# Sums of squares of k and q: ScalarE's accumulated squares against products with a column of ones

## The chip, the cores and the metric

One core of a Trainium2 chip runs the whole kernel. The metric is the device time of one execution in microseconds (us), here the median of three runs. Everything is in fp32; the large projections are made of split operands (fp32r), three products for one.

## What is computed

The reference is one layer with two request groups, 128 context tokens and 1024 latent tokens, which the kernel keeps side by side as nine chunks of 128 tokens (in rows of 1154 columns, with a gap of two between the groups). After an input projection it has a gated DeltaNet with 8 heads and an RG-LRU with 8 blocks. What the change touches is this part:

```python
def l2norm(x):
    return x * lax.rsqrt(jnp.sum(x * x, axis=-1, keepdims=True) + EPS)

def delta_branch(...):
    qkv = jax.nn.silu(short_conv(qkv, conv_w)).astype(jnp.float32)
    q, k, v = jnp.split(qkv.reshape(bsz, t, 3, N_DN_HEADS, DN_HEAD_DIM), 3, axis=2)
    q, k, v = l2norm(q[:, :, 0]), l2norm(k[:, :, 0]), v[:, :, 0]
```

For every token and head the sums of the 128 squares of k and of q are needed, with the tokens on the partitions, since the scales derived from them are applied to rows of tokens.

## The kernel before

**Layout.** k, q and v of a head are kept channel by channel: the 128 channels of the head on the partitions, the tokens along the row (`kT`, `qT`, `v_conv`, 1154 columns each). TensorE turns them to tokens chunk by chunk (`turn`, L741): three chunks to a PSUM bank, nine in all for one tensor, into banks 2, 3 and 4.

**Order of a head.** The loop over heads runs `joins(h)`, `scan(h)`, `phase_a(h)` on TensorE, ScalarE and VectorE, each engine with its own queue in order and with counted semaphores between them; one `phase_a(-1)` stands before the loop, so it runs eight times. `scan` goes through the nine chunks and is filled with projections of the next head. `phase_a` makes the next head's scores while TensorE does the other projections; meanwhile VectorE inverts 32 x 32 blocks (L1583 to L1592). `joins` combines the blocks.

**Sums of squares before.** In `phase_a` ScalarE copies the turned k to `ktok` (L1096) and squares each turned chunk from PSUM with a running sum (L1100), 9 squares, each followed by a readout of its accumulator. q is turned for nothing but this (L798): ScalarE squares its nine chunks with a running sum (L1143). The sums, `ssk` and `ssq`, go to VectorE (L1546 and L1631).

**Names in the steps.** L746 is the transposes, L784 the scores of phase_a, L673 to L675 the projections, L763 and L868 the products of the RG-LRU's gates, L824, L835 and L837 products of the joins. L1251 is the Silu that makes `qT` out of q's convolution, L1066 the squares of the output o, L992 the conversion of loaded weights (`w_hi`) whose rest VectorE makes (`w_lo`, L1379), L1104 the Silu of v, L1113 the exponentials of the decays, L1164 and L1604 the placing of inverted blocks. Weights come by `load_tile` (L441), which waits until an earlier projection is done. The memory `nmat` holds q's convolution (`q_conv`) until the Silu, and later the scaled scores.

Of the kernel before, what the change touches and what calls it, by code (L numbers as in the profile page):

```python
# [25 lines left out]
P = 128  # L26
# [31 lines left out]
def col(c):  # L58

    return 0 if c == 0 else GAP + P * c  # L60
# [42 lines left out]
def hybrid_layer(nc, x_prompt, x_sample, state_delta, state_rglru, c, c_ctx, ada_w, ada_b, pre_norm_w,  # L103
# [4 lines left out]
    with ctx:  # L108
        def sem(name):
# [11 lines left out]
            "ident": P, "head_cols": 280, "neg_Pk": INST,  # L121
# [55 lines left out]
        ident = view("ident")  # L177
        spare = at["rg"] + 2 * TW
# [20 lines left out]
        k_squares, q_squares, o_squares = view("sub", SQ, TOK), RH[:, 0:TOK], RC[:, 0:TOK]  # L199
# [76 lines left out]
        turned = Count(sem("turned"), 0, 9)  # L276
        turn_taken = Count(sem("turn_taken"), 0, 30)
# [256 lines left out]
        def _(gp):  # L534
# [10 lines left out]
            own(gp.memset(ones, 1.0))  # L545
            own(gp.memset(view("mask32"), 0.0))
# [93 lines left out]
        def _(pe):  # L640
# [100 lines left out]
            def turn(src, to):  # L741

                for n, bank in enumerate(to):
                    for i in range(3):
                        ch = 3 * n + i
                        mm = pe.transpose(banks[bank][:, P * i:P * i + P], src[:, col(ch):col(ch) + P], ident)  # L746
                    mm.then_inc(turned.sem, 1)

# [17 lines left out]
            def phase_a(b, first=False):  # L766
# [7 lines left out]
                turn(kT, (2, 3, 4))  # L774
# [4 lines left out]
                for f, bank in enumerate(SCORE_BANKS):  # L779
                    if f >= 3:  # L780
                        pe.wait_ge(turn_taken.sem, turn_taken.next(b, (4, 8)[f - 3]))
# [10 lines left out]
                pe.wait_ge(turn_taken.sem, turn_taken.next(b, 12))  # L792
# [4 lines left out]
                pe.wait_ge(turn_taken.sem, turn_taken.next(b, 21))  # L797
                turn(qT, (2, 3, 4))  # L798
# [7 lines left out]
            def joins(b, last=False):  # L806
                pe.wait_ge(turn_taken.sem, turn_taken.at(b, 30))
# [152 lines left out]
        def _(act):  # L960
# [101 lines left out]
            act.wait_ge(grounds_made, 1)  # L1062

# [27 lines left out]
            def phase_a(b, first=False):  # L1091

                for n in range(3):
# [4 lines left out]
                    for i in range(3):  # L1098
                        c1 = 3 * n + i
                        act.activation(k_squares[:, P * c1:P * c1 + P], ps[:, P * i:P * i + P], ACT.Square,  # L1100
                                       accum_out=hcc["ssk"][:, c1:c1 + 1]).then_inc(turn_taken.sem, 1)
# [37 lines left out]
                for n in range(3):  # L1139
                    act.wait_ge(turned.sem, turned.next(b, 6 + n + 1))  # L1140
                    for i in range(3):
                        c1 = 3 * n + i
                        act.activation(q_squares[:, P * c1:P * c1 + P], banks[2 + n][:, P * i:P * i + P], ACT.Square,  # L1143
# [679 lines left out]
```

## Time and profile before

| | us |
|---|---|
| median of 3 runs | 1523.67 |
| lowest and highest | 1518.97, 1530.37 |
| the profiled execution's own time | 1524.72 |
| its span, first to last instruction | 1523.1 |
| TensorE busy | 1391.1 |
| VectorE busy | 1027.9 |
| ScalarE busy | 753.3 |

Times in the trace are us from the span's start. PE is TensorE, DVE is VectorE, ACT is ScalarE, POOL is GpSimd. Busy times are those of recorded instructions; an instruction's time reaches to the end of its last write, so the next may start some 0.1 us before it ends. A line of the timeline may merge several instructions of one kind (x9). In brackets stands how long the engine was idle before a line, and who ended that. An fp32 product shows as two records, a transpose as one. The granted clock is TensorE's, as a share of full speed.

### The profile page before, as it was taken

The numbers are of one execution on the slowest core, as the hardware profiler recorded it, in microseconds if no ns is written. First come the engines' busy times: TensorE is split into PE (matmuls) and PEld (weight loads), VectorE is DVE, ScalarE is ACT, GpSimd is POOL, SyncE is SP. The second block draws the span as 40 slices with busy tenths as digits, with TensorE's granted clock in tenths as the row PEclk, the third lists the DMA queues.
The fourth block names the chain that finished last, engine by engine and source line by source line (L and its number), as shares of the span: only waits on it lengthen the run. The fifth ranks groups of instructions, "written<-read, shape, count | busy, mean of one in ns | idle before, by whom it ended". The sixth has DMA issues, their size and how long they took to land.

```text
span 1523.1 us, 24595 instructions
## 1 busy us (share of the span) xinstructions
PE 1391.1 (91%) x8182; PEld 1248.2 (82%) x8182; DVE 1027.9 (67%) x2135; ACT 753.3 (49%) x1912; POOL 115.3 (8%) x135
## 2 busy tenths in 40 slices
PE   5966899999999989999999999899989997599997
PEld 1266898899799879988997998799889976388886
DVE  3565477779677877887797778778877966722222
ACT  2351357564646465565647464745666484511111
POOL 0000100010001000100000010001000000212211
PEclk9978999999799999999999999999999998699999
DMA  8702111110111211111111111102111150523440
GB/s 306 249 14 68 28 29 32 57 44 30 40 49 44 57 48 28 60 33 42 44 44 36 53 44 49 55 22 67 33 42 45 44 225 20 153 77 110 124 123 29
DMA packets 95235, 102.79 MB, mean 67 GB/s; under 512 B 4230, under 2 KB 81271, under 8 KB 94089
## 3 DMA queue, kind: packets, MB, share of 16 engines
q1 hardware_dynamic: 92170, 90.70, 19.4%
q0 software_dynamic: 2944, 10.49, 1.8%
q8 instruction: 75, 1.23, 0.4%
q14 instruction: 46, 0.37, 0.1%
HBM read 85.88 MB, written 15.29 MB: 66 GB/s over the span
## 4 chain that ended last, share of the span: by engine, by line
PE 77%; ACT 8%; DVE 6%; issue 5%; DMA 3%; SPq 0%; DVEq 0%; ACTq 0%
PE bank L673 14%; PE bank L675 14%; PE bank L674 14%; PE bank L947 12%; PE bank L901 2%; PE bank L868 2%; PE bank L784 2%; PE bank L909 2%; PE bank L917 2%; PE bank L894 2%; PE bank L889 2%; PE bank L824 2%; DMA arena<-pos_row 2%; PE bank L746 1%; ACT L1089 1%
## 5 line engine op out<-in xcount | busy, mean ns | idle before, releaser
L673 PE MATMUL bank<-hT_hi,w_hi 128*128 128x384 f32 (+1 forms) x1224 | 442.0, 361 | 30.9 <-DVE w_lo L1379 17.6
L675 PE MATMUL bank<-hT_hi,w_lo 128*128 128x384 f32 (+1 forms) x1224 | 419.4, 343 | 0.0
L674 PE MATMUL bank<-hT_lo,w_hi 128*128 128x384 f32 (+1 forms) x1224 | 419.4, 343 | 0.0
L673 PEld LDWEIGHTS bank<-hT_hi,w_hi 128*128 128x128 f32 x1224 | 235.8, 193 | 33.7 <-DVE w_lo L1379 18.5
L674 PEld LDWEIGHTS bank<-hT_lo,w_hi 128*128 128x128 f32 x1224 | 235.9, 193 | 1.2
L675 PEld LDWEIGHTS bank<-hT_hi,w_lo 128*128 128x128 f32 x1224 | 234.9, 192 | 0.0
L1225 ACT ACTIVATE arena<-bank,arena 128x128 f32<-128x128 f32 x272 | 78.7, 369 | 176.2 <-PE bank L901 176.0
L1469 DVE SCALAR_TENSOR_TENSOR arena<-arena 128x1154 f32<-128x1154 f32 x96 | 137.5, 1433 | 3.5 <-DVE arena L1467 1.1
L947 PE MATMUL bank<-wo_hi,ot_hi 128*128 128x512 f32 x288 | 114.3, 397 | 18.8 <-DVE ot_lo L1758 13.5
L947 PE MATMUL bank<-wo_lo,ot_hi 128*128 128x512 f32 x288 | 113.6, 395 | 0.0
L947 PE MATMUL bank<-wo_hi,ot_lo 128*128 128x512 f32 x288 | 113.3, 393 | 0.0
L824 PE MATMUL bank<-arena 128*128 128x64 f32 x576 | 87.3, 289 | 4.1 <-issue 4.1
L824 PEld LDWEIGHTS bank<-arena 128*128 128x128 f32 x576 | 77.3, 201 | 15.7 <-issue 6.2
L1592 DVE TENSOR_TENSOR arena<-arena 128x30 f32<-128x30 f32 (+14 forms) x240 | 80.0, 333 | 8.2
L1590 DVE TENSOR_TENSOR arena<-arena 128x30 f32<-128x30 f32 (+14 forms) x240 | 79.6, 332 | 7.7
L1379 DVE TENSOR_TENSOR w_lo<-w_raw,w_hi 128x1024 fp32r<-128x1024 f32 x51 | 66.9, 1311 | 24.2 <-ACT w_hi L992 23.4
L947 PEld LDWEIGHTS bank<-wo_hi,ot_hi 128*128 128x128 f32 x288 | 54.9, 191 | 32.4 <-issue 19.7
L992 ACT ACTIVATE w_hi<-w_raw 128x1024 fp32r<-128x1024 f32 x51 | 54.8, 1075 | 50.8 <-DMA w_raw<-w_in 50.6
L1027 ACT ACTIVATE arena<-bank 128x384 f32<-128x384 f32 (+1 forms) x90 | 44.1, 490 | 72.0 <-PE bank L675 72.0
L1713 DVE TENSOR_TENSOR arena<-arena,bank 128x128 f32<-128x128 f32 x128 | 32.9, 288 | 66.8 <-PE bank L917 66.2
L868 PE MATMUL bank<-arena 128*128 128x386 f32 (+1 forms) x144 | 62.6, 536 | 9.2 <-ACT arena L1074 9.2
L1758 DVE TENSOR_TENSOR ot_lo<-ot,ot_hi 128x2048 fp32r<-128x2048 f32 x9 | 21.6, 2397 | 73.0 <-ACT ot_hi L1283 73.0
(224 smaller groups left out, 2388.4 us busy)
## 6 DMA issues: line engine op xcount, KB each, us to landing
w_raw<-w_in SPq DMA_DIRECT2D x51, 512.0 KB, 4.0
arena<-ada_w SPq DMA_DIRECT2D x8, 1536.0 KB, 10.8
arena<-scr_G SPq DMA_DIRECT2D x16, 576.0 KB, 4.8
ot<-scr_o SPq DMA_DIRECT2D x9, 1024.0 KB, 6.7
arena<-x_sample SPq DMA_DIRECT2D x16, 512.0 KB, 7.3
wo<-w_out SPq DMA_DIRECT2D x4, 2048.0 KB, 16.0
scr_o<-arena POOLq DMA_DIRECT2D x8, 576.0 KB, 4.2
arena<-pos_row SPq DMA_DIRECT2D x32, 128.0 KB, 5.5
```

The source lines that it names most:

```text
L673: pe.matmul(out, w_hi[:, slot, k], hT_hi[:, k, cols], start=first, stop=False)
L674: pe.matmul(out, w_hi[:, slot, k], hT_lo[:, k, cols], start=False, stop=False)
L675: return pe.matmul(out, w_lo[:, slot, k], hT_hi[:, k, cols], start=False, stop=last)
L824: mm = pe.matmul(bank[:, 64 * i:64 * i + 64], nmat[:, m], cols_in, start=True, stop=True)
L868: pe.matmul(banks[i % 2][:, 0:n], wg[:, 2 * of_input + d], xf[:, o:o + n], start=True, stop=True)\
L947: mm = pe.matmul(banks[2 * buf + half][:, :], a[:, buf, kk], b[:, k, cc], start=(k == 0 and i == 0), stop=(k == 15 and i == 2))
L992: act.activation(w_hi[:, slot], w_raw[:, slot], ACT.Copy).then_inc(w_hi_made.sem, 1)
L1225: act.activation(to[:, d], banks[2 + d][:, P:2 * P], ACT.Copy, scale=hcv[scale][:, d, c1])\
L1379: dve.tensor_tensor(w_lo[:, slot], w_raw[:, slot], w_hi[:, slot].bitcast(F32), ALU.subtract)\
L1469: step = dve.scalar_tensor_tensor(dest, raw[:, j % 2, t:t + TW], w, dest, ALU.mult, ALU.add)
L1590: own(dve.tensor_tensor(tmp, X[:, k + 1:, k:k + 1].to_broadcast([P, rows, k]), X[:, k:k + 1, 0:k].to_broadcast([P, rows, k]), ALU.mult))
L1592: own(dve.tensor_tensor(X[:, k + 1:, 0:k], X[:, k + 1:, 0:k], tmp, ALU.add))
```

## The change

The squares are made by ScalarE in one pass over the whole row, channel by channel (`vT` or `k_squares` from `kT`, `q_squares` from `qT`), and TensorE multiplies each chunk of 128 squared columns, as the weights, with a column of ones: nine products with one moving column give nine columns of sums in PSUM. For k they stand right behind the transposes and write into the free columns of bank 4; for q they take the place of the transposes. ScalarE copies the nine columns out. The squares of k move to the memory `nmat`, the squares of q stay in `RH` at full row length. ScalarE squares k behind the Silu of q at the end of `scan` (ahead of the loop behind the last weight conversion) and q where it squared the turned chunks before. TensorE gets two new waits, on `kq_squared`: one before it turns k, one before the sums of q.

```diff
-        k_squares, q_squares, o_squares = view("sub", SQ, TOK), RH[:, 0:TOK], RC[:, 0:TOK]
+        k_squares, q_squares, o_squares = view("nmat", 0, TW), RH, RC[:, 0:TOK]
...
-            def turn(src, to):
+            def turn(src, to, squares=None):
 
                 for n, bank in enumerate(to):
                     for i in range(3):
                         ch = 3 * n + i
                         mm = pe.transpose(banks[bank][:, P * i:P * i + P], src[:, col(ch):col(ch) + P], ident)
+                    if squares is not None and n == 2:
+                        mm = sum_squares(squares, banks[bank][:, 3 * P:3 * P + NCH])
                     mm.then_inc(turned.sem, 1)
+
+            def sum_squares(squares, out):
+                for ch in range(NCH):
+                    mm = pe.matmul(out[:, ch:ch + 1], squares[:, col(ch):col(ch) + P], one, start=True, stop=True)
+                return mm
...
-                turn(kT, (2, 3, 4))
+                pe.wait_ge(kq_squared.sem, kq_squared.next(b, 1))
+                turn(kT, (2, 3, 4), vT if first else k_squares)
                 project(48, 3, b)
...
                     if f >= 3:
-                        pe.wait_ge(turn_taken.sem, turn_taken.next(b, (4, 8)[f - 3]))
+                        pe.wait_ge(turn_taken.sem, turn_taken.next(b, f - 2))
...
-                pe.wait_ge(turn_taken.sem, turn_taken.next(b, 21))
-                turn(qT, (2, 3, 4))
+                pe.wait_ge(turn_taken.sem, turn_taken.next(b, 13))
+                pe.wait_ge(kq_squared.sem, kq_squared.next(b, 2))
+                sum_squares(q_squares, banks[2][:, 0:NCH]).then_inc(turned.sem, 1)
                 project(112, 16, b)
...
             high_w(0, 48)
             act.wait_ge(grounds_made, 1)
+            act.wait_ge(silued.sem, 1)
+            act.activation(vT, kT, ACT.Square).then_inc(kq_squared.sem, 1)
...
-                    for i in range(3):
-                        c1 = 3 * n + i
-                        act.activation(k_squares[:, P * c1:P * c1 + P], ps[:, P * i:P * i + P], ACT.Square,
-                                       accum_out=hcc["ssk"][:, c1:c1 + 1]).then_inc(turn_taken.sem, 1)
+                act.activation(hcc["ssk"], banks[4][:, 3 * P:3 * P + NCH], ACT.Copy).then_inc(turn_taken.sem, 1)
                 high_w(1, (w_loaded[1].at(b, 2) if not first else 4) * 16)
...
-                for n in range(3):
-                    act.wait_ge(turned.sem, turned.next(b, 6 + n + 1))
-                    for i in range(3):
-                        c1 = 3 * n + i
-                        act.activation(q_squares[:, P * c1:P * c1 + P], banks[2 + n][:, P * i:P * i + P], ACT.Square,
-                                       accum_out=hcc["ssq"][:, c1:c1 + 1]).then_inc(turn_taken.sem, 1)
+                act.activation(q_squares, qT, ACT.Square).then_inc(kq_squared.sem, 1)
                 for n in (14, 15):
                     take_projection(n, b)
+                act.wait_ge(turned.sem, turned.next(b, 7))
+                act.activation(hcc["ssq"], banks[2][:, 0:NCH], ACT.Copy).then_inc(turn_taken.sem, 1)
...
                     act.activation(qT, q_conv, ACT.Silu, scale=2.0).then_inc(silued.sem, 1)
+                    act.wait_ge(silued.sem, silued.at(b, 4))
+                    act.activation(k_squares, kT, ACT.Square).then_inc(kq_squared.sem, 1)
                 act.wait_ge(o_made.sem, o_made.at(b, 17))
                 square_o((2, 7, 1, 8), b)
```

The rest of the diff adjusts the counts of the semaphores (`turned` 9 to 7 per head, `turn_taken` 30 to 14) and makes the column `one`.

## Rows read from the trace of the kernel before

**Rows 1.** The page's chain that ended last, shares of the span by engine.

```profile
PE 77%; ACT 8%; DVE 6%; issue 5%; DMA 3%; SPq 0%; DVEq 0%; ACTq 0%
```

**Rows 2.** Busy us of each engine (x instructions) in two stretches of one head.

```profile
core 0: us, PE busy (x) PEld busy (x) DVE busy (x) ACT busy (x) POOL busy (x), PEclk, DMA share, GB/s
606.00:656.00 50.00, 50.00 (x297) 49.45 (x297) 43.41 (x101) 27.19 (x93) 4.68 (x8) 1.00 0.18 56
656.00:700.00 44.00, 37.49 (x257) 30.95 (x256) 33.69 (x58) 34.80 (x66) 0.00 (x0) 1.00 0.14 37
```

**Rows 3.** Timeline of TensorE: transposes of k in three heads.

```profile
321.63 1.15 PE L746 MATMUL bank<-arena 128*128 128x128 f32 x9
...
466.55 1.15 PE L746 MATMUL bank<-arena 128*128 128x128 f32 x9
...
606.26 1.15 PE L746 MATMUL bank<-arena 128*128 128x128 f32 x9
607.16 0.42 PE L673 MATMUL bank<-hT_hi,w_hi 128*128 128x386 f32 x1
```

**Rows 4.** Timeline of ScalarE, end of scan and start of phase_a.

```profile
606.40 1.16 ACT L1251 ACTIVATE arena<-arena 128x1154 f32<-128x1154 f32 x1
607.46 0.30 ACT L1066 ACTIVATE arena<-arena 128x128 f32<-128x128 f32 x1
...
608.64 0.47 ACT L1096 ACTIVATE arena<-bank 128x384 f32<-128x384 f32 x1
...
612.00 1.14 ACT L992 ACTIVATE w_hi<-w_raw 128x1024 fp32r<-128x1024 f32 x1
614.83 1.17 ACT L1104 ACTIVATE arena<-arena 128x1154 f32<-128x1154 f32 x1 [1.69 <-DVE arena L1469]
```

**Rows 5.** Timeline of TensorE in the joins.

```profile
670.46 0.78 PE L824 MATMUL bank<-arena 128*128 128x64 f32 x6
671.07 0.86 PE L868 MATMUL bank<-arena 128*128 128x384 f32 x2
```

**Rows 6.** Timeline of VectorE: the first score of phase_a taken.

```profile
618.13 0.65 DVE L1565 SCALAR_TENSOR_TENSOR arena<-bank,arena 128x128 f32<-128x128 f32 x2 [1.10 <-ACT arena L1113]
```

**Rows 7.** Timelines of TensorE and ScalarE about the transposes of q.

```profile
646.89 1.15 PE L746 MATMUL bank<-arena 128*128 128x128 f32 x9
...
647.09 0.49 ACT L1033 ACTIVATE arena<-bank 128x384 f32<-128x384 f32 x1 [2.98 <-PE bank L675]
647.48 0.27 ACT L1143 ACTIVATE arena<-bank 128x128 f32<-128x128 f32 x1
...
657.05 1.28 ACT L1258 ACT_TABLE_LOAD   x1
```

**Rows 8.** Timelines of the three engines at the start of the joins.

```profile
669.04 0.88 PE L824 MATMUL bank<-arena 128*128 128x64 f32 x6 [0.74 <-issue]
...
665.25 1.85 ACT L1164 ACTIVATE arena<-arena 32x288 f32<-32x288 f32 x4 [0.39 <-DVE arena L1595]
...
667.13 1.87 DVE L1604 COPY arena<-arena 32x288 f32<-32x288 f32 x4
```

**Rows 9.** Timelines of ScalarE and VectorE: a weight conversion in phase_a.

```profile
628.05 1.06 ACT L992 ACTIVATE w_hi<-w_raw 128x1024 fp32r<-128x1024 f32 x1 [2.60 <-DMA w_raw<-w_in]
...
630.88 1.22 DVE L1379 TENSOR_TENSOR w_lo<-w_raw,w_hi 128x1024 fp32r<-128x1024 f32 x1
```

**Rows 10.** Timelines of TensorE and ScalarE ahead of the loop.

```profile
168.31 0.60 PE L673 MATMUL bank<-hT_hi,w_hi 128*128 128x386 f32 x1 [2.78 <-DVE w_lo L1379]
...
182.59 1.14 PE L746 MATMUL bank<-arena 128*128 128x128 f32 x9
185.54 0.45 PE L673 MATMUL bank<-hT_hi,w_hi 128*128 128x386 f32 x1 [1.80 <-DVE w_lo L1379]
...
183.18 1.05 ACT L992 ACTIVATE w_hi<-w_raw 128x1024 fp32r<-128x1024 f32 x1
```

**Rows 11.** Busy us and granted clock (PEclk) behind those two gaps.

```profile
168.00:172.00 4.00, 3.69 (x12) 3.69 (x13) 3.90 (x4) 2.53 (x3) 0.00 (x0) 0.57 0.21 64
184.00:188.00 4.00, 2.46 (x13) 2.38 (x14) 3.67 (x4) 4.00 (x23) 0.00 (x0) 1.00 0.47 127
```

More of the change, by code:

```diff
@@ L119, in hybrid_layer @@
             "beta": NCH * 16, "eG": NCH * 16, "edec": NCH * 16, "gl": NCH * 16,
-            "ident": P, "head_cols": 280, "neg_Pk": INST,
+            "ident": P, "one": 1, "head_cols": 280, "neg_Pk": INST,
         }
@@ L177, in hybrid_layer @@
         ident = view("ident")
+        one = view("one")
         spare = at["rg"] + 2 * TW
@@ L275, in hybrid_layer @@
         silued = Count(sem("silued"), 3, 5)
-        turned = Count(sem("turned"), 0, 9)
-        turn_taken = Count(sem("turn_taken"), 0, 30)
+        turned = Count(sem("turned"), 0, 7)
+        turn_taken = Count(sem("turn_taken"), 0, 14)
+        kq_squared = Count(sem("kq_squared"), 0, 2)
         ss_done = Count(sem("ss_done"), 0, 2)
@@ L545, in _ @@
             own(gp.memset(ones, 1.0))
+            own(gp.memset(one, 1.0))
             own(gp.memset(view("mask32"), 0.0))
@@ L791, in phase_a @@
                 pe.wait_ge(scores_taken.sem, scores_taken.next(b, 28))
-                pe.wait_ge(turn_taken.sem, turn_taken.next(b, 12))
+                pe.wait_ge(turn_taken.sem, turn_taken.next(b, 4))
                 turn(v_conv, (2, 3, 4))
@@ L806, in joins @@
             def joins(b, last=False):
-                pe.wait_ge(turn_taken.sem, turn_taken.at(b, 30))
+                pe.wait_ge(turn_taken.sem, turn_taken.at(b, 14))
                 pe.wait_ge(oz_made.sem, oz_made.prev(b, 4))
@@ L1543, in phase_a @@
                     mean_o(b)
-                dve.wait_ge(turn_taken.sem, turn_taken.next(b, 12))
+                dve.wait_ge(turn_taken.sem, turn_taken.next(b, 4))
                 own(dve.tensor_scalar(hcc["ssk"], hcc["ssk"], EPS, None, ALU.add))
@@ L1629, in joins @@
                     if slot == 10:
-                        dve.wait_ge(turn_taken.sem, turn_taken.at(b, 30))
+                        dve.wait_ge(turn_taken.sem, turn_taken.at(b, 14))
                         dve.tensor_scalar(hcc["epsq"], hcc["ssq"], P * EPS, P * EPS * EPS, ALU.mult, ALU.add)\
```

## The prediction, made before the changed kernel ran

> **What bounds the kernel now.** I read the page first, then the busy times of two stretches of one head, then the timelines of TensorE, ScalarE and VectorE through that head. Of the chain that ended last, 77% is TensorE's, ScalarE has 8% and VectorE 6% [rows 1]; so a wait or an instruction of TensorE is likely to be on the path, and one of ScalarE is not, until shown. The two stretches say where. From 606 to 656 us (the end of a head's scan and phase_a) TensorE is busy in all 50.00 us while ScalarE works 27.19 of 50. From 656 to 700 us (the gates and the joins) no engine is full: TensorE 37.49 of 44, ScalarE 34.80, VectorE 33.69 [rows 2]. The changed instructions all stand in or just before phase_a, where TensorE has no gap and ScalarE has many. The reader is to see in the timelines which instruction of TensorE stands where a new wait will be.
>
> The head between the transposes of k at 466.55 and those at 606.26 took 139.71 us, the one before, from 321.63, 144.92 us [rows 3]. I use the head that begins at 606.26 as the pattern and count phase_a eight times: once ahead of the loop and seven times in it.
>
> **The wait on the squares of k.** Today TensorE turns k to tokens as soon as the scan's last product is out: nine transposes in 606.26 to 607.16, 0.90 us [rows 3]. After the change they stand behind a wait for the whole of k squared by ScalarE. ScalarE cannot start that early: the squares go into the memory that q's convolution held, so they wait for the Silu of q, which runs from 606.40 for 1.16 us, to 607.56 [rows 4]. A pass over 1154 columns takes 1.17 us here (the Silu of v) [rows 4]; the square ends at about 608.76, and with some 0.05 us for the signal TensorE goes on at 608.81. That is a stall of 608.81 - 606.26 = **2.55 us**. Nothing hides it: TensorE's queue is in order, and behind the wait stand the transposes, all of phase_a's projections and the scores.
>
> **The products with the column of ones, k.** Nine fp32 products follow the transposes. An fp32 product is two records here. The trace of before has none with one moving column; the nearest is the join's product with 64 moving columns and 128 columns of weights, six records from 670.46 to the next line at 671.07, 0.102 us each [rows 5]. The transposes, with twice the moving columns, take 0.10. Twice the columns at the same price says that the load of the weights sets the pace, and the squares are the weights here. So I take 0.102: 18 x 0.102 = **1.84 us**. Bounds: nothing (0.0) if all of that price were columns, and 0.13 if the records didn't overlap at all (0.78 us for six, counted to the end of the last) [rows 5], so 0 to 2.3 us for nine.
> The Trainium skill (TensorE: Matmul & The Clock Gate, Back-to-back issue gap) lets a matmul of 1 to 64 columns go at its issue floor of about 25 ns; the same page (LDWEIGHTS) puts a load at columns / 1.2, about 107 ns for 128. By the first 18 records would be an estimated 0.45 us, and the whole sum below about 22 us smaller (rival C); the row with 64 columns already contradicts it and sides with the second, though no run here has one column.
>
> **What ScalarE gains there, and why it buys nothing.** Behind Silu q ScalarE has four squares of o (607.46), then three copies and nine squares with their readouts (608.64 to 612.00), then a weight conversion, and then it stands idle 1.69 us for VectorE before Silu v at 614.83 [rows 4]. Three copies at about 0.37 us leave 3.36 - 1.11 = 2.25 us for the squares. The new order is the long square (1.07), squares of o (1.18), copies, one copy of nine sums (0.12): TensorE delivers the last bank and the sums at 608.81 + 0.90 + 1.84 = 611.55, so the conversion starts near 612.1 instead of 612.0 and is over before 614.83. Silu v, the decays behind it and VectorE's first use of a score at 618.13 [rows 6] don't move; the scores themselves come about 4.4 us later than now but still before that, as they start near 613.2. The score banks wait for the copies alone, no longer for squares; that isn't a wait that ends last either.
>
> **The squares of q.** TensorE now turns q at 646.89 without any wait. The new wait is for a square that ScalarE begins only after it has taken the projection that TensorE has just finished: take at 647.09, the next instruction at 647.48 [rows 7]. The square, a pass of the same 1154 columns, ends at 647.48 + 1.17 = 648.65, TensorE goes on at 648.70: a stall of **1.81 us**, though ScalarE had long been idle. Then nine products with ones instead of nine transposes: 1.84 - 0.90 = **0.94 us** (bounds -0.90 to +1.4). ScalarE saves nine squares here (2.25 us), has the long one instead, and later one more small copy ahead of the table load at 657.05 [rows 7], about **0.12 us** more before the gates, for which TensorE waits.
>
> **Does the delay survive up to the joins?** At the joins the three engines meet. TensorE stood idle 0.74 us before 669.04, so it had finished at 668.30. ScalarE's first blocks of Zt were placed by 665.25 + 1.85 = 667.10; VectorE's blocks of Z, needed only one step later, by 667.13 + 1.87 = 669.00 [rows 8]. So TensorE comes last and has no slack to take up a delay. VectorE gets later as well: the weights are loaded when a projection is done, so the conversion at 628.05, which waited 2.60 us for its DMA, moves by 2.55 + 1.84 = 4.39 us, to 632.4 to 633.5, and VectorE, which wants it at 630.88 [rows 9], is 2.6 us late. Its later conversion comes no later than that. 2.6 is less than TensorE's own 7.3 us, so it costs nothing; with a short TensorE delay it would count in its place. The joins and the scan then only shift.
>
> Sum per head in the loop: 2.55 + 1.84 + 1.81 + 0.94 + 0.12 = 7.26 us, seven times 50.8. In the first phase_a TensorE has a gap today: transposes at 182.59, then a wait for weights until 185.54 [rows 10]. The square follows the conversion at 183.18 (1.05 us) and ends near 185.30, so TensorE turns k from 185.35, does the ones until 188.09 and is 2.55 us late; with the q part 2.87 that is 5.4. Together **56.2 us** on the profiled execution's own 1524.72 us (span 1523.1), which is 1.05 us above the median of the runs: 1580.9.
>
> **The clock.** A gap of 2.78 us before 168.31 was followed by a granted clock of 0.57 on average from 168 to 172, that is the lower level, 1.2 GHz, for most of the time; it costs 4 x 0.43 = 1.7 us of full-speed work, of which 0.1 fell on a gap: 1.6. The gap of 1.80 us before 185.54 left it at 1.00 [rows 10, 11]. The new stall at k, 2.55 us, lies near the first, and nine transposes and nine one-column products follow it, in which the array streams little; the stall at q, 1.81, is like the second but has thin products behind it. I count five falls of 16 stalls, 8 us: **1589 us**. No fall gives 1581, a fall at each 1524.7 + 56.2 + 16 x 1.6 = 1606.5.
> The Trainium skill (TensorE: Matmul & The Clock Gate, Part 1: The HAM clock gate) says that the throttled state is the default and activity releases it. The trace agrees: 0.57 behind the longer gap.
>
> **Rivals.**
> A. The forecast: both stalls and the products on the path, and the clock falls behind some of them: 1576 to 1602.
> B. The clock falls behind nearly every stall: about 1606. For it: the thin work behind each. Against: 185.54.
> C. The price of a product falls with its columns, at most from 0.102 to about nothing: 36 records less by up to 0.102 is 3.7 us per head, 29 us less, 1560 with the same clock. For it: one column against 64. Against: 64 and 128 columns cost the same. The issue floor of the Trainium skill's page named above would put it at an estimated 1567.
> D. No stall, because the square runs inside a gap of ScalarE that I have missed (TensorE later than I think at both places): only the products remain, (1.84 + 0.94 + 0.12) x 8 = 23 us, 1548. Against: at 606.26 and at 646.89 TensorE starts before ScalarE has the input free.
> E. The other side: ScalarE, not TensorE, sets phase_a. It loses 18 squares with readouts (4.5 us) and gets 2.3 us, so 2.2 us less per head: 1524.7 - 17.6 = 1507, faster. It decides only if TensorE is more than 7.3 us ahead of ScalarE when the joins start; the rows have TensorE last, by 1.2 us. If the others merely tied with it, the result would be near 1524.
>
> **How the numbers follow.** A 0.68, B 0.10, C 0.11, D 0.06, E with its tie 0.05. The prediction is A's 1589. A and what the bounds of the products allow around it, with half of C and B up to its 1606, give 1564 to 1607 for 8 in 10. About 1%, 15 us, is what a measurement of this kernel can tell from no change. Slower by over 1%: A, B, C and D, 0.95 less 0.01 for smaller sizes of D, so 0.94; within 1% 0.03; faster 0.03.
>
> **What would show it.** In the profile after: a wait of TensorE of about 2.5 us before the transposes of k, released by ScalarE's Square, eight times; one of about 1.8 us before the ones of q, released by its Square; the two-record products at 0.10 us; ScalarE 2.2 us less busy per head; VectorE idle about 2.6 us at the conversion that reads w_lo's inputs; a head of 147 to 150 us between the transposes of k; a granted clock under 1.00 behind some stalls of k. I am wrong if those waits are short, if TensorE stands before the joins for another engine, or if a head is less than 3 us longer.

## The result, and the profile after

| | before | changed |
|---|---|---|
| median of four executions, us | 1523.16 | 1653.07 |
| lowest and highest | 1518.97, 1530.37 | 1638.83, 1665.01 |
| profiled execution: span, us | 1523.1 | 1663.4 |
| its mean granted clock | 0.960 | 0.911 |

The ratio is 1.082 with a 95% interval of 1.072 to 1.092: the changed kernel is 8% slower, far above the forecast of 1589 and its range of 1564 to 1607. The profiled execution of the changed kernel is the longest of its four and counts as a slow one, so the ratio is made from the other three, whose clocks were 0.918 to 0.930. What follows from the trace is therefore about a difference of 140 us between the two profiled executions (1665.0 and 1524.7 us); for the other three the difference to the median before is 116 to 136 us. The heads, from one turn of k to the next, took 155.0 to 161.8 us.

Both waits are there. These are waits of TensorE in the changed kernel: who waited for whom, us in total, times, the longest.

```profile
PE bank L749 <- ACT arena L1261: 16.7, 7, 2.4
PE bank L756 <- ACT arena L1150: 13.2, 8, 1.7
...
PE bank L880 <- issue: 9.0, 6, 1.8
```

L749 is the transposes, L756 the products with ones, L1261 and L1150 the long squares of k and q. An eighth wait at k, ahead of the loop, is 2.67 us. The third line is new as well, in the joins (below). The timeline of TensorE around one turn of k, beside [rows 3]:

```profile
814.69 2.18 PE L749 MATMUL bank<-arena 128*128 128x128 f32 x9 [2.39 <-ACT arena L1261]
816.66 3.83 PE L756 MATMUL bank<-arena 128*128 128x1 f32 x18
820.36 0.67 PE L676 MATMUL bank<-hT_hi,w_hi 128*128 128x386 f32 x1
```

The nine transposes, 0.90 us in [rows 3], took 1.97 here, and the eighteen records of the products 3.70. That is the clock; columns as in [rows 11], PEclk the third from the right:

```profile
812.00:816.00 4.00, 1.61 (x9) 1.42 (x8) 3.85 (x5) 3.97 (x12) 0.11 (x1) 0.79 0.48 131
816.00:820.00 4.00, 4.00 (x22) 4.00 (x20) 3.60 (x3) 0.67 (x2) 1.75 (x5) 0.50 0.37 147
820.00:824.00 4.00, 4.00 (x14) 3.91 (x14) 2.77 (x8) 2.56 (x4) 0.00 (x0) 0.50 0.00 0
824.00:828.00 4.00, 4.00 (x21) 3.64 (x20) 0.00 (x0) 0.00 (x0) 0.00 (x0) 0.93 0.00 0
...
862.00:866.00 4.00, 2.37 (x19) 2.23 (x18) 3.66 (x11) 1.55 (x2) 0.00 (x0) 0.94 0.00 0
866.00:870.00 4.00, 4.00 (x14) 4.00 (x14) 3.69 (x10) 0.00 (x0) 0.00 (x0) 0.50 0.00 0
...
1046.00:1066.00 20.00, 19.61 (x80) 16.26 (x81) 8.52 (x13) 10.42 (x23) 0.00 (x0) 0.51 0.01 1
```

The clock fell to its lower level, 1.2 GHz, during the stall of k and stayed there for some 10 us; it fell behind the stall of q (863.77), and it was low for some 20 us in joins (the last row). This is one of the two longest falls at k: in the other six heads the clock fell 1.0 to 2.3 us after the stall's end, so that the transposes ran at full clock (1.01 to 1.04 us) and the products took 2.54 to 3.68 us.

**How the 140 us divide.** Mean clock and span give the time at the lower level, 2 x (1 - clock) x span: 122 us before, 296 us in the changed kernel. For an engine that is busy throughout, work at half the clock takes twice as long, and half of the difference, 87 us, would be the clock's. The rest, span x clock, went from 1462.2 to 1515.4, 53 us; in the other three executions to 1520 to 1523, 58 to 61 us. The forecast had 56.2 us for this part and 8 us for the clock.

This division is a frame and not a measurement, and 87 us is an upper bound. Half is right behind the stalls, where TensorE was idle in only 0.6 of 92 us of low time. In the joins TensorE waits for other engines at full clock, and at the lower one it works through some of these waits. [rows 3] price it: the head of 144.92 us had 20.5 us more low time in its joins than the head of 139.71 us and was 5.2 us longer, a quarter. Over 112 executions of all kernels, each compared with executions of the same kernel only, 1 us more of low time goes with 0.32 us more time (a straight line; it gives 0.14 to 0.47 for single kernels). An estimate from these: 46 us behind the stalls, 20 to 25 us in the joins, and some 64 us for the stalls, the products and gaps.

Added up over its falls, the low time of the changed kernel lies 37 us ahead of phase_a (as before), 92 us behind the sixteen stalls (61 at k, 31 at q; none before), 130 us in the joins (51 before), and 37 us after the last joins (34 before). So every stall was followed by a fall, and the joins had more low time too. These two are what the experiments are about.

### The profile page after: what moved, and what is told of

The parts are those of the page before. It is cut to its first block, busy times and chain, and to the rows that moved or that the text cites. A ratio compares the mean times of both kernels' runs of the same rounds, so it can differ in the third digit from the quotient of the medians.

```text
span 1663.4 us, 24787 instructions
## 1 busy us (share of the span) xinstructions
PE 1500.2 (90%) x8398; PEld 1343.2 (81%) x8398; DVE 1030.9 (62%) x2135; ACT 738.6 (44%) x1656; POOL 115.1 (7%) x136
## 4 chain that ended last, share of the span: by engine, by line
PE 80%; ACT 7%; DVE 6%; issue 4%; DMA 2%; SPq 0%; ACTq 0%; DVEq 0%
PE bank L676 14%; PE bank L678 13%; PE bank L677 13%; PE bank L959 11%; PE bank L836 4%; PE bank L880 3%; PE bank L756 3%; PE bank L795 2%; PE bank L847 2%; PE bank L913 2%; PE bank L901 2%; PE bank L906 2%; PE bank L921 2%; PE bank L929 2%; PE bank L849 1%
## 5 line engine op out<-in xcount | busy, mean ns | idle before, releaser
L676 PE MATMUL bank<-hT_hi,w_hi 128*128 128x384 f32 (+1 forms) x1224 | 451.2, 369 | 29.1 <-DVE w_lo L1389 15.8
L678 PE MATMUL bank<-hT_hi,w_lo 128*128 128x384 f32 (+1 forms) x1224 | 427.5, 349 | 0.0
L677 PE MATMUL bank<-hT_lo,w_hi 128*128 128x384 f32 (+1 forms) x1224 | 427.4, 349 | 0.0
L676 PEld LDWEIGHTS bank<-hT_hi,w_hi 128*128 128x128 f32 x1224 | 242.7, 198 | 31.7 <-DVE w_lo L1389 16.5
L677 PEld LDWEIGHTS bank<-hT_lo,w_hi 128*128 128x128 f32 x1224 | 242.8, 198 | 1.2
L836 PE MATMUL bank<-arena 128*128 128x64 f32 x576 | 100.2, 320 | 5.7 <-ACT arena L1172 4.2
L836 PEld LDWEIGHTS bank<-arena 128*128 128x128 f32 x576 | 89.3, 228 | 18.6 <-ACT arena L1172 5.4
L1039 ACT ACTIVATE arena<-bank 128x384 f32<-128x384 f32 (+1 forms) x90 | 44.5, 494 | 126.8 <-PE bank L678 126.8
L1575 DVE SCALAR_TENSOR_TENSOR arena<-bank,arena 128x128 f32<-128x128 f32 x144 | 42.3, 345 | 89.3 <-ACT arena L1124 88.6
L880 PE MATMUL bank<-arena 128*128 128x386 f32 (+1 forms) x144 | 75.7, 635 | 15.5 <-issue 9.0
L1045 ACT ACTIVATE arena<-bank 128x384 f32<-128x384 f32 (+1 forms) x48 | 23.3, 486 | 134.2 <-PE bank L678 134.2
```

What stands on the lines that cost most here:

```text
L676: pe.matmul(out, w_hi[:, slot, k], hT_hi[:, k, cols], start=first, stop=False)
L677: pe.matmul(out, w_hi[:, slot, k], hT_lo[:, k, cols], start=False, stop=False)
L678: return pe.matmul(out, w_lo[:, slot, k], hT_hi[:, k, cols], start=False, stop=last)
L836: mm = pe.matmul(bank[:, 64 * i:64 * i + 64], nmat[:, m], cols_in, start=True, stop=True)
L880: pe.matmul(banks[i % 2][:, 0:n], wg[:, 2 * of_input + d], xf[:, o:o + n], start=True, stop=True)\
```

## The experiments

Each kernel's executions were compared with executions of the kernel before that ran beside them ("before"; its median moved between 1522.9 and 1530.8). "Low" is the mean over a kernel's executions of 2 x (1 - clock) x span, "full" the mean of span x clock; "stalls" and "joins" are the low times of its one trace between 184 us and the last joins, outside the joins and in them (42 us from their first product with 64 moving columns). All in us. The expectations quote counts from a rougher cut (118 for e6 in the joins, 55 and 71 for the two traces of the kernel before), and the 99 us in two of them is too low: the mean clock of that trace gives 122.

```
kernel            median  before   low  full  stalls  joins
before, 1st trace 1523.2     -     122  1462     0     51
changed           1653.1  1523.2   262  1520    92    130
e1 stall only     1574.2  1530.8   166  1489    17     75
e2 no stall       1575.4  1530.8   165  1491     0     58
e3 filled         1599.2  1530.8   169  1514     7     85
e4 before again   1528.2  1530.8   128  1462     3     67
e5 k part         1591.5  1525.0   195  1493    75     72
e6 q part         1590.7  1525.0   223  1478    41    123
e7 k split        1571.6  1525.0   160  1489    20     75
e8 joins filled   1530.3  1525.0   123  1467     0     41
e9 q filled       1576.6  1522.9   187  1480    17     85
e10 q split       1559.9  1522.9   149  1482     3     79
e11 q long stall  1577.2  1522.9   169  1491    48     31
e12 pad of 4      1564.5  1527.9   192  1462     3    130
e13 pad of 8      1560.9  1527.9   140  1488     3     51
e14 pad of 12     1590.9  1527.9   176  1500     0     82
```

### The stall, the thin products, or both: e1, e2, e3

e1 is the kernel before with the long squares as extra work and the waits for them:

```diff
+                pe.wait_ge(kq_squared.sem, kq_squared.next(b, 1))
                 turn(kT, (2, 3, 4))
...
+                pe.wait_ge(kq_squared.sem, kq_squared.next(b, 2))
                 turn(qT, (2, 3, 4))
```

> The kernel before with the two waits alone: ScalarE makes the long squares of k and of q in addition to its old work, nobody reads them, and TensorE waits for them before it turns k and before it turns q. No product with ones. The stalls measured in the changed kernel are 2.39 and 1.63 us; eight of each are 32 us, so 1523 + 32 = 1555 without any effect on the clock. Theory U (the stalls make the clock fall, in phase_a and then in the joins): the time at the lower clock grows from 99 us to well over 200, 50 to 80 us more, 1605 to 1635. Theory V (the thin one-column products make it fall): time at the lower clock stays near 100, about 1557. Theory B (both are needed, the stall and the thin work behind it): between, 1557 to 1585.

It took 1574.2 us, 1.029 times before (1.025 to 1.032). The stalls cost what they last (full +29). Five of the eight stalls of k were followed by a fall, of 3.4 us each, and none of q's eight. U had wanted 50 to 80 us from the clock; the low time grew by about 31 us, 10 to 16 us of time. U is out as stated.

e2 is the changed kernel with its products where their squares are ready:

```diff
-                pe.wait_ge(kq_squared.sem, kq_squared.next(b, 1))
-                turn(kT, (2, 3, 4), vT if first else k_squares)
+                turn(kT, (2, 3, 4))
...
                     if f == 2:
+                        pe.wait_ge(turn_taken.sem, turn_taken.next(b, 3))
+                        pe.wait_ge(kq_squared.sem, kq_squared.next(b, 1))
+                        sum_squares(vT if first else k_squares, banks[4][:, 3 * P:3 * P + NCH]).then_inc(turned.sem, 1)
                         project(51, 5, b)
```

and for q behind `project(112, 8, b)`. ScalarE's copy of the sums of k moves behind its weight conversion with them.

> The changed kernel with its products moved to where their squares are ready: those of k behind the first six chunks' scores, those of q eight units of projection later. All instructions stay, both stalls of TensorE go. Work on the path: 288 records at 0.107 less 72 transposes at 0.10 is 24 us, so 1547 without the clock. Theory U (stalls): time at the lower clock back to about 100 us, 1545 to 1560. Theory V (thin products): it stays at 200 or more, 1600 to 1625. Theory B (both needed): as U.

1575.4 us, 1.032 times before (1.025 to 1.040), and 78 us less than the changed kernel with the same instructions. No fall stands behind the products in any of the eight heads, for k or for q: V is out. Its timeline and clock at the products of k:

```profile
770.82 2.06 PE L756 MATMUL bank<-arena 128*128 128x1 f32 x18
772.74 0.42 PE L676 MATMUL bank<-hT_hi,w_hi 128*128 128x386 f32 x1
...
770.00:776.00 6.00, 6.00 (x41) 5.84 (x40) 5.50 (x10) 3.01 (x6) 1.30 (x4) 1.00 0.26 101
```

Eighteen records in 1.92 us, 0.107 each at the full clock. The time is still 15 to 30 us above what was expected. About 10 us of it is a gap of TensorE in the joins that no other engine ends (its waits have "PE bank L883 <- issue: 10.1, 6, 2.1"), the rest goes with the clock in two of four executions (1584 and 1586 us at 0.938 and 0.936, against 1566 us at 0.958); where in them it was low no trace shows.

e3 keeps the waits of the changed kernel and gives TensorE work without use in them:

```diff
+                for _ in range(6):
+                    pe.matmul(banks[5][:, 0:256], kT[:, 0:P], kT[:, 0:256], start=True, stop=True)
                 pe.wait_ge(kq_squared.sem, kq_squared.next(b, 1))
                 turn(kT, (2, 3, 4), vT if first else k_squares)
...
+                for _ in range(4):
+                    pe.matmul(banks[3][:, 0:256], qT[:, 0:P], qT[:, 0:256], start=True, stop=True)
                 pe.wait_ge(kq_squared.sem, kq_squared.next(b, 2))
```

> The changed kernel with products without use in both stalls (six and four fp32 products of 256 columns, about 2.6 and 1.7 us, into a free bank), so that TensorE works where it stood idle; the waits and everything behind them stay where they are. If the clock does not matter the time is 1653 again or a few us more. Theory U: the falls in phase_a and joins go, time at the lower clock about 100 us, 1523 + 58 = 1581 to 1595. Theory V: the falls stay, 1640 to 1660.

1599.2 us: work without use made the changed kernel 54 us faster. Its full time is close to that of the changed kernel (1514 against 1520); the low time behind the stalls went from 92 to 7 us, two falls of 3.4 us behind the filled stall of q. A stretch with the filled stall, the transposes and the products:

```profile
780.17 2.76 PE L785 MATMUL bank<-arena 128*128 128x256 f32 x12
782.76 1.17 PE L749 MATMUL bank<-arena 128*128 128x128 f32 x9
783.77 2.07 PE L756 MATMUL bank<-arena 128*128 128x1 f32 x18
...
780.00:792.00 12.00, 12.00 (x75) 11.20 (x75) 10.12 (x15) 7.23 (x17) 1.86 (x5) 1.00 0.29 94
```

The reader is to see 1.00 over a stretch in which the thin work is all there. So the cause that is left for most of the falls is B: a stall with thin work directly behind it.

### The kernel before again: e4

The kernel is unchanged.

> The kernel before once more, for the spread of its clock: one trace has 99 us at the lower clock, 44 of them in the loop over heads. If falls in the joins are a matter of chance, another execution shows another number of long falls there (each some 20 us, 10 us of time), and the times of the kernel spread accordingly; the four times so far spread over only 11 us, so I expect at most one long fall more or less, 1515 to 1535.

1520.95 to 1535.98 us in ten executions. The trace had one long fall in its fourth joins (23.9 us) and two of 13.7 and 6.8 us close together in the last joins, where the first trace had one long fall, in its second joins. So falls in the joins come by chance also in the kernel before, and the times follow the clock, 0.951 at the slow end and 0.965 at the fast.

The trace also corrects the reading of [rows 10] and [rows 11]. The same gap of 1.80 us ahead of the loop, with the same instructions behind it, is followed by a fall here:

```profile
186.08 0.45 PE L673 MATMUL bank<-hT_hi,w_hi 128*128 128x386 f32 x1 [1.80 <-DVE w_lo L1379]
...
188.00:192.00 4.00, 4.00 (x15) 3.38 (x13) 3.83 (x9) 2.01 (x4) 0.00 (x0) 0.67 0.00 0
```

Eleven of the traces have this gap; a fall of 3.4 us follows it in seven (e4, e6, e9 to e13) and none in four. One trace's answer to "does the clock fall behind this gap" is one draw.

### One part at a time, and the stall and the products apart: e5, e6, e7, e10

e5 leaves out the part for q, e6 the part for k:

```diff
 e5, for q as before
-                sum_squares(q_squares, banks[2][:, 0:NCH]).then_inc(turned.sem, 1)
+                turn(qT, (2, 3, 4))
 e6, for k as before
-                turn(kT, (2, 3, 4), vT if first else k_squares)
+                turn(kT, (2, 3, 4))
```

> The change for k alone; q is turned and squared as before. At full clock: stalls 7 x 2.39 + 0.9 and products 8 x 1.92 make 33 us. In the changed kernel's trace the clock was low for 61 us behind the eight stalls of k, 30 us of time. If the parts add (theory B: a stall followed directly by thin products), 1526 + 33 + 30 = 1589, with up to 15 more from the joins; if the falls need both parts of the change, about 1560.

> The change for q alone. At full clock: stalls 8 x 1.64 and products for transposes 8 x (1.92 - 0.99) make 20.5 us. Behind the stalls of q the clock was low for about 31 us in the changed kernel, 15 us of time. Theory B, parts add: 1526 + 20.5 + 15 = 1562, with up to 15 more from the joins. If a stall of 1.64 us is too short for a fall by itself and the falls behind it came from what the k part had left: about 1547.

e5 took 1591.5 us, as expected: full +31, and a fall behind each of the eight stalls, 6.8 or 10.2 us. e6 took 1590.7 us where 1562 was expected: full +16, all eight stalls of q followed by a fall too (3.4 or 6.8 us), and 123 us of low time in the joins. So a stall of 1.64 us is long enough, if the products stand behind it; in e1 the same stall had the nine transposes behind it and there was no fall.

e7 and e10 keep the instructions of e5 and e6 and move the products away from the stall (in e7 also ScalarE's copy of the sums, behind its weight conversion, and a wait for the copies of the turned k comes ahead of the products):

```diff
 e7, against e5
-                turn(kT, (2, 3, 4), vT if first else k_squares)
+                turn(kT, (2, 3, 4))
...
                     if f == 2:
+                        pe.wait_ge(turn_taken.sem, turn_taken.next(b, 3))
+                        sum_squares(vT if first else k_squares, banks[4][:, 3 * P:3 * P + NCH]).then_inc(turned.sem, 1)
 e10, against e6
                 pe.wait_ge(kq_squared.sem, kq_squared.next(b, 1))
+                project(112, 8, b)
                 sum_squares(q_squares, banks[2][:, 0:NCH]).then_inc(turned.sem, 1)
-                project(112, 16, b)
+                project(120, 8, b)
```

> The change for k alone as in the last but one, with the stall kept ahead of the transposes, but the nine products with ones moved 4.1 us back, behind three units of projection and six chunks' scores. Stall, transposes, products and all other work are the same. Theory B (it is the stall with thin work directly behind it, nine transposes and eighteen records in one stretch): falls behind k go from 61 us of low clock to under 15, 1526 + 33 + 5 = 1564. If stall and thin work count wherever they stand in the head: as the run with the k part, 1589.

> The q part alone with its stall where it was (1.64 us) but the nine products eight units of projection later; instructions and length at full clock as in the q part. Theory B (a stall with thin work directly behind it makes the fall): no fall behind q. Then J expects the joins back to 40 to 85 us and 1545 to 1560; K expects as many long falls in the joins as in the q part, 1570 to 1590.

e7: 1571.6 us, 20 less than e5, low behind the stalls 20 us instead of 75. e10: 1559.9 us, 31 less than e6, nothing behind the stalls instead of 38 (the 3 us are the gap ahead of the loop). Granted clocks and timelines, first of e5, then of e7:

```profile
629.11 2.18 PE L749 MATMUL bank<-arena 128*128 128x128 f32 x9 [2.39 <-ACT arena L1263]
631.08 3.83 PE L756 MATMUL bank<-arena 128*128 128x1 f32 x18
...
628.00:640.00 12.00, 10.89 (x43) 10.52 (x44) 8.75 (x13) 5.65 (x15) 1.86 (x5) 0.57 0.26 88
```

```profile
913.70 1.83 PE L749 MATMUL bank<-arena 128*128 128x128 f32 x9 [2.39 <-ACT arena L1266]
917.91 2.75 PE L795 MATMUL bank<-arena 128*128 128x256 f32 x12
920.50 2.06 PE L756 MATMUL bank<-arena 128*128 128x1 f32 x18
...
620.00:632.00 12.00, 9.75 (x63) 9.43 (x64) 9.86 (x14) 6.66 (x16) 1.86 (x5) 1.00 0.28 93
912.00:924.00 12.00, 10.30 (x57) 9.98 (x58) 8.30 (x13) 6.23 (x16) 1.86 (x5) 0.86 0.28 93
```

With the products directly behind, e5 has 0.57 over twelve us; with them apart, e7 has one short fall (0.86) or none (1.00). For q this is B: no fall with the products apart, eight with them. For k it is B in part. Six of the eight stalls of k in e7 were still followed by a fall, and five of eight in e1, of 3.4 us each; the products right behind made it eight of eight (e5) and two or three times as long. No run has projections directly behind the stall of k, so whether 2.39 us of idle time suffice or the transposes are needed too stays open.

### What lengthens the low time in the joins: e8, e9, e11, and the pads e12 to e14

e8 fills two gaps of TensorE in the joins of the kernel before:

```diff
+                    if i == 11:
+                        fill_gap(3)
                     pe.wait_ge(gate_tanh.sem, gate_tanh.at(b, i - 1))
...
+                fill_gap(3)
                 pe.wait_ge(dZ_taken.sem, dZ_taken.at(b, 30))
```

> The kernel before with three products without use (256 columns, 1.3 us) in each of two gaps of TensorE in the joins, ahead of its last gate (idle 1.40 us) and ahead of the scan (idle 1.53 us); nothing that TensorE does later depends on them. If TensorE's idle stretches decide whether the clock falls in the joins, its low time there (55 and 71 us in two traces of the kernel before) shrinks to under 30 and the kernel gains up to 20 us, 1505 to 1515. If the thin 64-column products alone decide, no change: 1520 to 1535.

1530.3 against 1525.0 us, ratio 1.003 (1.000 to 1.006): no gain, low time 123 against 125 us in the kernel before, 5 us more work. These two gaps do not decide the sum. In its trace the falls that start 24 to 32 us into the joins, behind these gaps (five in the first trace of the kernel before), are gone, while those that start at 16 to 17 us are there.

e9 fills the stall of q in e6 as e3 does. e11 is the kernel before with a wait of TensorE for three long squares ahead of the transposes of q:

```diff
+                pe.wait_ge(kq_squared.sem, kq_squared.next(b, 3))
                 turn(qT, (2, 3, 4))
```

> The q part alone with four products without use (256 columns, about 1.7 us) in its stall. The trace of the q part had a fall behind each of its eight stalls (3.4 to 6.8 us) and then long falls in the joins, 118 us there, four of eight joins at 18 us or more; over both the changed kernel and the q part that was 9 of 16 joins, and 5 of 64 in the traces that had no fall behind q. Theory J (a fall behind q, some 30 us ahead of the joins, brings the long falls there): without the falls of q the joins are back to 40 to 85 us and the kernel to 1524 + 18 + 10 = 1545 to 1560. Theory K (the joins' falls come with how the head's length lies to the chip, not with the fall of q): low time in the joins stays about 118, 1570 to 1590.

> The kernel before, with a wait of TensorE ahead of the transposes of q for three long squares of ScalarE that nobody reads: a stall of about 4.0 us and no product with ones. At full clock 8 x 4.0 = 32 us more. The stall should bring a fall in each head by its length alone (one of 2.8 us did ahead of the loop). Theory J: long falls (18 us or more) in about half of the joins, low time there near 118, so 1526 + 32 + 8 x 1.7 + 30 = 1600. Theory K: joins as in the kernel before, 1526 + 32 + 14 = 1572.

e9 took 1576.6 us, 14 less than e6, with 85 us in the joins, but two of eight joins had a long fall again; between J and K, inconclusive. It also limits B: with the stall filled TensorE had no idle time there, and yet four of eight products of q were followed by a fall of 3.4 us (two of eight in e3). Behind eight units of projection (e2, e10) none was. e11 speaks against J: its stall (4.03 us) brought a fall in every head, 48 us outside the joins, and the joins had 31 us, the least of all traces, with no long fall. Stall and clock behind it, then one of its joins:

```profile
668.83 1.71 PE L747 MATMUL bank<-arena 128*128 128x128 f32 x9 [4.03 <-ACT arena L1144]
...
668.00:676.00 8.00, 7.17 (x35) 7.17 (x36) 7.35 (x20) 3.35 (x20) 0.00 (x0) 0.79 0.00 1
700.00:742.00 42.00, 37.76 (x262) 33.89 (x262) 29.06 (x51) 25.40 (x55) 3.24 (x4) 0.92 0.12 38
```

The pads are the kernel before with 4, 8 or 12 products more in each phase_a, at a place where TensorE is busy anyway:

```diff
                 pe.wait_ge(turn_taken.sem, turn_taken.next(b, 21))
+                for _ in range(4):
+                    pe.matmul(banks[3][:, 0:256], kT[:, 0:P], kT[:, 0:256], start=True, stop=True)
```

> The kernel before with four products without use (256 columns, 0.43 us each, 1.7 us) ahead of the transposes of q in each phase_a: no wait, no idle stretch and no one-column product is added, TensorE is only busy longer, and a head longer. At full clock 8 x 1.73 = 14 us. Theory K (how long the head is decides where the joins lie to the chip's measuring of the load, and so the falls in them): total low time differs from the 109 to 166 us of the kernel before, and between the three runs of this kind, by 30 us or more. Theory L (only idle or thin stretches of phase_a bring more falls in the joins): total low time 110 to 150, time 1537 to 1545.

> As the run before with eight such products, 3.5 us a head, 28 us in all at full clock. Theory L: total low time 110 to 150 again, 1550 to 1560. Theory K: another total than with four, by 30 us or more in one of the three.

> As the run before with twelve such products, 5.2 us a head, 41 us in all at full clock. Theory L: total low time 110 to 150, 1564 to 1574. Theory K: as above; by the part for q (5 us longer heads than these and no more idle time in the joins) it could reach 200, 1595 to 1605.

Low times were 192, 140 and 176 us. The pad of twelve had 152 to 198 us in its four executions, and the kernel before beside it 112 to 150; no idle time was added. The pad of four fell apart into two groups: one execution took 1538 us with 120 us of low time, as L had it, and three took 1562 to 1569 us with 203 to 226 us. In the trace of one of the longer ones all eight joins had a fall, 130 us together. Two of its joins, and one of the kernel before:

```profile
678.00:720.00 42.00, 40.32 (x225) 33.73 (x226) 25.61 (x36) 27.22 (x57) 1.29 (x3) 0.72 0.18 58
968.00:1010.00 42.00, 40.02 (x223) 33.44 (x224) 25.61 (x36) 27.41 (x58) 0.84 (x2) 0.72 0.21 60
```

```profile
669.00:711.00 42.00, 37.17 (x262) 32.20 (x263) 29.56 (x45) 28.33 (x62) 3.24 (x4) 0.96 0.22 64
```

L is out by the pad of twelve, whose low time (176 us) and time (1590.9 us) lie above L's 110 to 150 and 1564 to 1574: more busy work alone can bring more low time. K's differences of 30 us came too, but one kernel (the pad of four) gave 120 and 226 us, so the length of a head does not settle it for one execution, and that it matters at all is not shown.

The changed kernel's own trace says more about its joins. Four of its five long falls there (20.5 us each) begin 3.8 to 4.1 us after the joins' first product, at the end of the new gap of TensorE before L880:

```profile
411.08 0.88 PE L836 MATMUL bank<-arena 128*128 128x64 f32 x6 [1.04 <-ACT arena L1172]
411.80 0.86 PE L880 MATMUL bank<-arena 128*128 128x386 f32 x2
412.50 0.78 PE L836 MATMUL bank<-arena 128*128 128x64 f32 x6
415.08 1.65 PE L880 MATMUL bank<-arena 128*128 128x384 f32 x2 [1.80 <-issue]
...
411.00:431.00 20.00, 18.12 (x86) 15.57 (x86) 9.32 (x14) 9.72 (x23) 0.00 (x0) 0.60 0.10 28
```

The gap was 1.80, 1.81, 1.70 and 1.54 us long in these four joins and 1.05 us in two others, where no fall followed it at once. In e2 it was followed by a long fall where it was longest (2.12 and 2.14 us) and by none at 1.05 to 1.84 us. In e6 three of four long falls begin within 1.5 us of a wait of 1.79 to 2.25 us before the joins' first product. In the traces of all other kernels but e9 no fall of the joins begins before 15.7 us. So 82 of the changed kernel's 130 us stand behind a short stall with products of 64 columns around it, which looks like B once more. No run takes this gap away and leaves the rest, so this is argued and not shown, and why the gap is there is open; so is how much of the 130 us is chance. If the falls behind the stalls are alike in all four executions (229 to 296 us in all, less 92 and about 74 outside the heads), the joins had some 63 to 130 us.

## Why the prediction was wrong, by its steps

- **Who is on the path, and the waits.** Right. Stalls of 2.39 us (2.55 foretold; 2.67 ahead of the loop) and 1.64 us (1.81), eight of each. A head is 155.0 to 161.8 us long instead of the foretold 147 to 150, and ScalarE is 1.8 us less busy per head (753.3 to 738.6 us in all) instead of 2.2.
- **The products with ones.** Right in price: 0.107 us a record (0.102 foretold). The price doesn't fall with the moving columns: 64 of them cost 0.102 in [rows 5], one 0.107, so rival C fell. That the load of the 128 weight columns sets it fits; no run varied these. The issue floor of the Trainium skill (TensorE: Matmul & The Clock Gate, Back-to-back issue gap), about 25 ns, is not what a pair of load and product costs here; the same page's LDWEIGHTS section (107 ns for 128 columns, by its formula) agrees with the trace.
- **The sum without the clock.** 56.2 us foretold; 53 measured in the profiled execution, 58 to 61 in the others. Terms at the full clock: stalls at k 19.4 less the gap of 1.8 that was there before [rows 10], stalls at q 13.2, products of k 8 x 1.92, products for transposes at q 8 x (1.92 - 0.90), gates 0.5, together 54.8; and one I had not: up to 9.0 us of gaps before L880 in the joins that no engine ends. They are in e2 (10.1) but not in e3, e5, e6 or e7, so neither part brings it by itself; what it is stays open. 54.8 and 9.0 are more than 53; TensorE's waits for the other engines at the gates and blocks of the joins went from 17.8 us (L868, L835) to 10.8 (L880, L847), and span x clock counts low time in the joins as if TensorE had been full.
- **What doesn't move in phase_a.** Wrong, without a price. I had Silu v and the decays in place. Silu v was, but ahead of the decays ScalarE takes a projection, and TensorE was late with it. VectorE in the changed kernel, beside [rows 6]:

```profile
831.70 0.65 DVE L1575 SCALAR_TENSOR_TENSOR arena<-bank,arena 128x128 f32<-128x128 f32 x2 [8.34 <-ACT arena L1124]
...
891.03 0.36 DVE L1629 TENSOR_TENSOR arena<-bank,arena 128x192 f32<-128x192 f32 x1 [7.74 <-PE bank L836]
```

  It waited 8.34 us for the decays, and still 7.74 us for TensorE at the joins: TensorE came later than VectorE there, as foretold, because it was later still. Against ScalarE the margin was gone: in four of the eight joins TensorE stood idle 1.00 to 1.10 us before its first product until ScalarE had placed its blocks (L1172; the row at 411.08 above), where the trace before has 0.46 to 0.92 us, in six joins, that no engine ends.
- **The clock.** The step that failed: "I count five falls of 16 stalls, 8 us." There were sixteen, and they were longer. I priced one by a stall with full work behind it [rows 11], 3.4 us of low time. Behind a stall of k it is 6.8 or 10.2 us, behind one of q 3.4 or 6.8. 92 us of low time, 46 us, instead of 8. I had leaned on the idle time as the measure (2.78 us fell, 1.80 did not). The second half of that was one draw: the same gap of 1.80 us was followed by a fall in seven of eleven traces. What decides whether and how long the clock falls is the work behind the stall: nine transposes behind 1.64 us brought no fall (e1), the products eight of eight (e6), projections none (e10), and at k the products made falls of 3.4 us into falls of 6.8 and 10.2 (e7 against e5).
- **The joins.** Not in the forecast at all: the term was nothing. [rows 3] showed it: heads of 139.71 and 144.92 us with the same work, which I noted and did not put into the range. The kernel before alone took 1515 to 1539 us over all its executions, and its low time was 106 to 166 us. With 79 us more low time in the joins than in the trace before, they made an estimated 20 to 25 us of the profiled execution's 140. Four of the eight joins also had the new gap, with 82 us of low time behind it.
- **Rival B** had the right sign and the wrong unit: a fall at each stall at 1.6 us a fall is 26 us, with the measured lengths it is 46. The Trainium skill (TensorE: Matmul & The Clock Gate, HAM oscillation) tells of a kernel whose waits made each group of products start at the lower clock, and takes half of the low time as the loss. This trace agrees with the first: sixteen of sixteen. Half is borne out where TensorE was busy, behind the stalls; over all executions it was 0.32, and a quarter in [rows 3].

No version tried was faster than the kernel before. With its stalls gone the change still puts 288 records at 0.107 us on an engine that was full and takes 1.8 us a head from one that was not.

## What to carry to other kernels

Before a wait is put in front of an engine that is full, look for when the waited result can be ready, and put work there that does not need it: the same instructions cost 1575 us with the products moved behind and 1653 us without. Price a stall of TensorE by what stands behind it, and keep one-column products away from the restart. Whether the clock falls behind a given gap is to be read from several executions and not from one. Where the granted clock of equal stretches already differs in the trace of before, that spread belongs into the range of any change to the length of the loop.

## What was not expected of the hardware

- A useless product in a stall paid: 80 products of 256 columns in the stalls took 54 us off (e3 against the changed kernel).
- A stall of 1.64 us with nine transposes behind it was followed by no fall in eight heads (e1), with nine products of one column by eight in eight (e6), with projections by none (e10). With the stall filled by products of 256 columns the one-column products were still followed by a fall in six of sixteen (e3, e9).
- 5.2 us of busy work more in each head, with no idle time, went with 152 to 198 us at the lower clock instead of 112 to 150 (e14).
- The lower clock costs less than half of its time where TensorE waits for other engines: 20.5 us more of it in one head's joins cost 5.2 us.
